# Half a token block moved in two feed-forward phases, early gate columns, and a third token-stationary input in the recurrent block

## The reference

```python
# every feed-forward layer
jnp.square(jax.nn.relu(x @ w1)) @ w2

# second block, layer 0 (recurrent)
h = _modulate(_rmsnorm(x, norm_g[layer]), shift, scale)
u, g = jnp.split(h @ w_in, 2, axis=-1)
u = causal_conv4(u) + conv_b
r  = sigmoid(_block_diag(u, w_a) + b_a)
gi = sigmoid(_block_diag(u, w_x) + b_x)
log_a = -RG_C * r * softplus(-lam)
a = exp(log_a)
b_in = sqrt(-expm1(2.0 * log_a)) * (gi * u)
hs = scan(a, b_in)                  # over tokens
y = (hs * silu(g)) @ w_out
x = x + gate[:, None, :] * y
```

## Time and profile before

| | us |
|---|---|
| median of 3 runs | 780.31 (780.28 to 780.37) |
| the profiled execution, its own time | 780.2 |
| its span in the profile | 778.4 |
| PE busy | 768.9 (99%) |
| PEld busy | 697.1 (90%) |
| DVE busy | 586.1 (75%) |
| ACT busy | 405.1 (52%) |
| POOL busy | 34.6 (4%) |

### The profile page before, as it was taken

How to read it: one execution, slowest core, us unless ns; L and a number is a source line. 1 busy time by engine, 2 the same in 40 slices (tenths; PEclk the granted TensorE clock), 3 DMA queues, 4 the chain that set the end, 5 groups by cost and what they waited for, 6 DMA issues and landing times.

```text
span 778.4 us, 12084 instructions
## 1 busy us (share of the span) xinstructions
PE 768.9 (99%) x4982; PEld 697.1 (90%) x4982; DVE 586.1 (75%) x786; ACT 405.1 (52%) x512; POOL 34.6 (4%) x66
## 2 busy tenths in 40 slices
PE   9999999999999999999999999999999999999996
PEld 9999888988998889888889988998799988999995
DVE  5886898868688697687989776676687877756754
ACT  5455235545445424875355444445649869664632
POOL 0000000000000001000000000000500051000001
PEclk9999999999999999999999999999999999999999
DMA  9877438897867731446488977876235254754102
GB/s 351 319 274 278 184 125 324 348 320 289 313 231 288 290 122 62 163 139 267 165 326 344 347 273 275 308 263 245 103 109 216 109 216 163 270 216 164 55 3 80
DMA packets 26983, 173.94 MB, mean 223 GB/s; under 512 B 3248, under 2 KB 3632, under 8 KB 7856
## 3 DMA queue, kind: packets, MB, share of 16 engines
q1 hardware_dynamic: 26640, 173.14, 60.0%
q10 hardware_dynamic: 288, 0.02, 0.0%
HBM read 172.10 MB, written 1.05 MB: 222 GB/s over the span
## 4 chain that ended last, share of the span: by engine, by line
PE 93%; DVE 3%; ACT 2%; POOL 1%; issue 0%; POOLq 0%; ACTq 0%
PE bank L578 12%; PE bank L580 12%; PE bank L579 12%; PE Y L714 10%; PE Y L716 10%; PE Y L713 10%; PE bank L1067 2%; PE bank L1068 2%; PE bank L1069 2%; PE bank L996 2%; DVE w_low L1610 1%; PE bank L816 1%; PE Y L738 1%; PE bank L610 1%; PE bank L619 1%; PE bank L611 1%
## 5 line engine op out<-in xcount | busy, mean ns | idle before, releaser
L1610 DVE TENSOR_TENSOR w_low<-raw,w_high 128x2048 fp32r<-128x2048 f32 (+3 forms) x125 | 278.5, 2238 | 65.1 <-ACT w_high L1203 62.8
L1203 ACT CAST w_high<-raw 128x2048 fp32r<-128x2048 f32 (+3 forms) x125 | 232.5, 1869 | 92.9 <-DMA raw<-weights 80.0
L578 PE MATMUL bank<-xT_h,w_high 128*128 128x256 f32 x728 | 206.5, 284 | 0.1
L579 PE MATMUL bank<-xT_l,w_high 128*128 128x256 f32 x728 | 205.8, 283 | 0.0
L580 PE MATMUL bank<-xT_h,w_low 128*128 128x256 f32 x728 | 205.8, 283 | 0.0
L578 PEld LDWEIGHTS bank<-xT_h,w_high 128*128 128x128 f32 x728 | 139.4, 192 | 1.6 <-DVE w_low L1610 0.3
L579 PEld LDWEIGHTS bank<-xT_l,w_high 128*128 128x128 f32 x728 | 139.4, 191 | 1.1
L580 PEld LDWEIGHTS bank<-xT_h,w_low 128*128 128x128 f32 x728 | 139.5, 192 | 0.0
L714 PE MATMUL Y<-w_low,hT_h 128*128 128x512 f32 x324 | 128.3, 396 | 0.0
L713 PE MATMUL Y<-w_high,hT_h 128*128 128x512 f32 x324 | 128.0, 395 | 0.0
L716 PE MATMUL Y<-w_high,hT_l 128*128 128x512 f32 x324 | 101.9, 395 | 0.0
(11 more groups left out here) (291 smaller groups left out, 1144.5 us busy)
## 6 DMA issues: line engine op xcount, KB each, us to landing
raw<-weights SPq DMA_DIRECT2D x149, 1024.0 KB, 5.0
rows<-rows_in SPq DMA_DIRECT2D x9, 512.0 KB, 7.7
raw<-weights SPq DMA_DIRECT2D x4, 576.0 KB, 3.5
z<-gates_in SPq DMA_DIRECT2D x4, 512.0 KB, 3.8
raw<-weights SPq DMA_DIRECT2D x2, 896.0 KB, 4.4
raw<-weights SPq DMA_DIRECT2D x3, 512.0 KB, 7.0
x<-x_in SPq DMA_DIRECT2D x2, 512.0 KB, 4.4
kT<-rows_in SPq DMA_DIRECT2D x2, 512.0 KB, 8.3
```

Of the source, the lines that this page charges most:

```text
L578: mm(dst, high, xh[:, kt, :], start=kt == 0, stop=False)
L579: mm(dst, high, xl[:, kt, :], start=False, stop=False)
L1203: nc.scalar.copy(w_high[:, n % RING, start:COLS[n]], raw[:, s % RAW, start:COLS[n]]).then_inc(w_high_ready, 1)
L1610: tt(w_low[:, n % RING, start:COLS[n]], slot[:, start:COLS[n]], f32(w_high[:, n % RING, start:COLS[n]]), ALU.subtract).then_inc(raw_done, 1)
```

## The change

PE, feed-forward: the first half of group 2 for block 0 is issued ahead of the transposes of block 1, and the first half of group 2 for block 1 ahead of `turn_pair(0)`. This holds for `ff0` and `ff1`.

Gate columns of layer 0: POOL makes all eight in `raw_columns`, in `ff1` behind the square of unit 0, with the bias added in the same instruction. PE turns them into rows right behind the transposes of `rs1` block 0, and ACT copies the rows ahead of the scaling of block 1. DVE's bias addition waits for the columns.

Third input: u2 is made with the tokens as the stationary side, block 0 behind the transposes of block 1, and block 1 behind u1. Then `turn_input(2)` turns it. Its weight split moves on DVE from behind the staging of block 1 to ahead of the layer norm of block 1, behind a wait for POOL's root of `rs1` block 0.

Exit: ACT and DVE split v1 and v2 one place earlier than before, and ACT also v3.

```diff
@@ unit_table
-    t.extend([("gate", 0, 0), ("gate", 0, 1), ("rg", "u", 0), ("rg", "u", 1)])
+    t.extend([("gate", 0, 0), ("gate", 0, 1), ("rg", "u", 0), ("rg", "u", 1), ("rg", "u", 2)])
@@ PE, feed_forward
                 pair_block(first[0], phase, 0, fresh)
+                up_block(first[2], PI[phase, "up", 2], 0, fresh, range(0, KT // 2))
                 transposes(fresh, x, "x_ready", [1])
-                up_block(first[2], PI[phase, "up", 2], 0, fresh)
+                up_block(first[2], PI[phase, "up", 2], 0, fresh, range(KT // 2, KT))
                 pair_block(first[1], phase, 1, fresh)
+                up_block(first[2], PI[phase, "up", 2], 1, fresh, range(0, KT // 2))
                 turn_pair(phase, 0)
                 in_order(phase, 2)
-                up_block(first[2], PI[phase, "up", 2], 1, fresh).then_inc(product, 1)
+                up_block(first[2], PI[phase, "up", 2], 1, fresh, range(KT // 2, KT)).then_inc(product, 1)
@@ PE, recurrent block
             transposes("rs1", z, blocks=[0], z_name="rs1")
+            for n in range(2):
+                gate_row(0, n)
...
             transposes("rs1", z, blocks=[1], z_name="rs1")
-            for n in range(2):
-                gate_row(0, n)
+            inputs.append(open_unit("rg", "u", 2))
+            up_block(inputs[2], PI["rg", "u", 2], 0, "rs1")
...
             up_block(inputs[1], PI["rg", "u", 1], 1, "rs1", quarter[1]).then_inc(product, 1)
+            in_order("rg", "u", 2)
+            up_block(inputs[2], PI["rg", "u", 2], 1, "rs1", quarter[0])
+            turn_input(1)
+            up_block(inputs[2], PI["rg", "u", 2], 1, "rs1", quarter[1]).then_inc(product, 1)
...
-            input_tile(2, 0, quarter[0])
-            turn_input(1)
-            input_tile(2, 0, quarter[1])
             for g in range(1, MXG + 1):
                 if g == 2:
-                    input_tile(2, 1).then_inc(u_ready, 1)
+                    turn_input(2)
@@ POOL
+            def raw_columns():
+
+                pool.wait_ge(S["token_hidden"], nth("token_hidden", "ff1", 0))
+                pool.wait_ge(raw_done, AT["mod", MOD["gate0"] // 2 + KT // 2 - 1] + 1)
+                for t in range(KT):
+                    last = nc.gpsimd.tensor_scalar(area_f[:, t * P:(t + 1) * P], ones[:, :], mcol("gate0", t),
+                                                   col("mod_b", MOD["gate0"] + t), ALU.mult, ALU.add)
+                last.then_inc(columns_ready, 2)
...
+            raw_columns()
             roots("ln3", "rs1", blocks=[0])
-            pool.wait_ge(mod_ready, 1)
-            repeated_columns(0, 0)
             first_low("rs1", 0)
             roots("ln3", blocks=[1])
             for part in (1, 2, 3):
                 first_low("rs1", part)
             roots("rs1", blocks=[1])
-            repeated_columns(0, 1)
+            pool.wait_ge(mod_ready, 1)
@@ ACT
             rms_squares("rs1", "ln3", 1)
+            act.wait_ge(S["x_ready"], nth("x_ready", "ln3", 2 * TB - 1))
+            for n in range(2):
+                await_product(act, "gate", 0, n)
+                nc.scalar.copy(rows[:, 0, n * 512:(n + 1) * 512], bank_of("gate", 0, n)[:, :]).then_inc(evacuates("gate", 0, n), 1)
             rms_scale("rs1", 1, [0])
...
-            split_ahead(("rg", "down", MXG - 1), 2)
+            split_ahead(("rg", "down", MXG - 1), 3)
             rms_squares("rs2", "rg", 0)
...
-            split_ahead(("rg", "down", MXG - 1), 3)
+            split_ahead(("rg", "down", MXG - 1), 4)
             gate_kept(0)
             rms_squares("rs2", "rg", 1)
-            split_ahead(("rg", "down", MXG - 1), 4)
@@ DVE
             def modulation_parameters():
+                dve.wait_ge(columns_ready, 2)
...
             layer_norm_apply("ln3", 0)
             modulation_parameters()
+            await_rstd("rs1", 0)
+            split_ahead(("ff1", "down", FFG - 1), 4)
             layer_norm_sums("ln3", "ff1", 1)
...
             split_transposed("rs1", 1, *modulation["rs1"])
-            split_ahead(("ff1", "down", FFG - 1), 4)
...
-            split_ahead(("rg", "down", 3), 1)
+            split_ahead(("rg", "down", 3), 2)
             gated_residual("rg", 0, 0)
             await_rstd("rs2", 0)
-            split_ahead(("rg", "down", 3), 2)
+            split_ahead(("rg", "down", 3), 3)
```

More of the change, by code:

```diff
@@ L953, in turn_input @@
                         last = nc.tensor.transpose(u_bank(g)[:, t * SEQ + b * P:t * SEQ + (b + 1) * P],
-                                                   buf_a[:, g, b * SEQ + t * P:b * SEQ + (t + 1) * P], ident)
+                                                   buf_a[:, g % 2, b * SEQ + t * P:b * SEQ + (t + 1) * P], ident)
                 last.then_inc(u_ready, 1)
@@ L1457, in gate_tanhs @@
                 last.then_inc(evacuates("rg", kind, i), 1)
-            def gate_copied(n):
-                await_product(act, "gate", 0, n)
-                nc.scalar.copy(rows[:, 0, n * 512:(n + 1) * 512], bank_of("gate", 0, n)[:, :]).then_inc(evacuates("gate", 0, n), 1)
             def input_copied(g):
                 await_product(act, "rg", "u", g)
-                nc.scalar.copy(buf_a[:, g, :], bank_of("rg", "u", g)[:, :]).then_inc(evacuates("rg", "u", g), 1)
-            act.wait_ge(S["x_ready"], nth("x_ready", "ln3", 2 * TB - 1))
-            for n in range(2):
-                gate_copied(n)
+                if g >= 2:
+                    act.wait_ge(u_ready, g - 1)
+                nc.scalar.copy(buf_a[:, g % 2, :], bank_of("rg", "u", g)[:, :]).then_inc(evacuates("rg", "u", g), 1)
             split_ahead(("rg", "g", 1), 0)
@@ L1473, in _ @@
             input_copied(1)
+            input_copied(2)
             def output_gate(i):
```

## The result

| | before | changed |
|---|---|---|
| median, us | 780.34 (780.28 to 780.44) | 783.76 (783.64 to 784.3) |
| profiled execution, us | 780.2 | 783.7 |
| its span, us | 778.4 | 781.9 |

The ratio is 1.0044, with a 95% interval of 1.0033 to 1.0056: slower by 3.4 us, where 2.8 were forecast. Timed once more beside the experiments the changed kernel came to 1.0036 (1.0024 to 1.0049).

The account below looks back on a forecast made before the run. It took PE as the bound (busy 99%, 93% of the chain of waits). `ff0` 0.48, `ff1` 0.73, recurrent block 1.5 and POOL's columns 0.1 summed to +2.8 us on 780.2: 783.0 us, range 779.0 to 784.9.

Parts of the forecast that it names:

- Feed-forward: `ff0` and `ff1`: DVE's list behind the later transposes ends later and delays `down` of block 1, +0.48 and +0.73 us.
- Columns in `ff1`: `ff1`: POOL's eight `raw_columns` instructions beside DVE's closed list cost +0.1 us, bounds 0 and 1.2 us.
- Rival 3: POOL's lock delays two modulation products in `ff1` (0.6 us each) and exit columns (some 0.3): 784.4 us, chance 0.12.
- Entry: Entry of the recurrent block, to g0: +2.12 us, including −1.31 gate rows, +1.09 early split, +2.88 u2 matmuls.
- The chain hangs on a0: Recurrent block: ACT and DVE's chain is 2.12 us later throughout; `down` (3,0) starts +0.85 us, with a wait of 1.4.
- Exit: Exit: two DVE splits ahead of the gated residual delay it 2.20 us and PE's transposes +1.9 us, 0.85 already counted.
- the root follows by 4.34 us as before: Exit: the root comes 4.34 us behind the gated residual's start, unchanged from the kernel before.
- The wait for v2's split: Exit: the earlier split on ACT removes PE's wait for v2's remainder, −0.4 us.
- The sum: Whole kernel: 0.48 + 0.73 + 1.5 + 0.1 = +2.8 us, 783.0 us; chance 0.52.
- Rival 1: Whole kernel: PE alone decides, since the lists have more air than read; −2.6 us, 777.6 us, chance 0.13.
- Rival 2: Feed-forward gains 0.6 and the block costs 1.5 (781.1 us), or feed-forward costs 1.2 and the block nothing (781.4); chance 0.23.

Follow-up runs that it names:

- Experiment 1: The kernel before with the half-block moves in feed-forward alone: 781.62 us, ratio 1.0014.
- experiment 2: The changed kernel with DVE's silu moved ahead of the remainders of block 1 in `ff1`, into DVE's wait for ACT: 782.58 us, ratio 1.0027.
- experiment 12: The changed kernel as it is, timed again: 783.32 us, ratio 1.0036.
- Experiment 11: The changed kernel with POOL's `first_low` part 1 ahead of its root of `ln3` block 1 at the entry: 783.36 us, ratio 1.0036.
- Experiments 7: The changed kernel without the third input, u2 made and split as in the kernel before: 781.45 us, ratio 1.0014.
- experiment 9: The changed kernel with group 0 in the order a0 x0 g0, on PE, ACT and DVE: 780.71 us, ratio 1.0.
- experiment 5: The changed kernel with ACT's and DVE's weight splits at the exit put back as before: 782.9 us, ratio 1.003.
- experiment 3: The changed kernel without DVE's wait for POOL's root of `rs1` block 0 ahead of u2's split: 785.24 us, ratio 1.0057.
- experiment 4: The changed kernel with u2's split behind the layer norm of block 1, and without the wait for POOL's root: 784.94 us, ratio 1.0059.
- experiment 6: The changed kernel with POOL's root of `rs2` block 0 between the two groups of four gate columns of layer 1: 786.39 us, ratio 1.0076.
- experiment 10: The changed kernel with a0 x0 g0, silu ahead of the remainders in `ff1`, exit splits and `ff0` as before: 779.66 us, ratio 0.9988.

## Why the forecast held, and where it was off

**Feed-forward: right, and shown.** The steps gave 0.48 and 0.73 us, and measured were 0.47 and 0.67. Experiment 1 has them alone (1.1 us), and experiment 2 shows that the list on DVE carries the one of `ff1`. The wait of 0.5 us for the square wasn't foreseen. It takes nothing more, because `down` of block 1 waits for the end of the same list anyway.

**Columns in `ff1`: 0.1 too much.** `raw_columns` took 7.53 us for eight instructions (9.57 in the trace of experiment 12), but DVE's modulation products beside it lasted 1.22 us as before, and the waits of experiment 1 are the same without it. POOL did the waiting. Rival 3 fails in this half.

**Entry: right in size.** The sum to g0 was +2.12 us. a0 came 2.04 later (28.57 − 26.53), with the wait of 1.04 us for `first_low` part 1 that was named at 1.1. Experiment 11 adds a point that the step had wrong in form: it put the cost at POOL's order. That order only decides where the wait is met. The layer norm behind the early split holds both.

**The chain hangs on a0: right.** The last remainder was to be 2.12 us later and was 2.06. `down` (3,0) started 0.80 us later than the entry explains, where the forecast had 0.85; PE's wait there was 1.05 us and not 1.4. Experiments 7 and 9 move a0 in the other direction, and the remainder follows.

**Exit: the mechanism was right, a term too small.** Of the transposes the forecast said +1.9 us, and they came 2.50 late. The step that failed is "the root follows by 4.34 us as before": from the start of the residual to the split that waits for the root it was 4.95 us (641.00 to 645.95). The root was not waiting for ACT's squares but for the columns ahead of it on POOL, held up by a third split of DVE. That is the half of rival 3 that came true, at 0.6 us and not 0.3. The kernels agree: the columns lasted 11.03 us with three splits beside them and 8.97 with two, and 8.89 with two in experiment 5. With two, the root had 1.50 us to spare in the kernel before and 0.35 in experiment 5. The wait for v2's split is gone, and the stretch to the end is 0.4 us shorter, as the step said.

**The sum.** The terms of one execution are 0.47 + 0.67 in the phases, 0.24 of small shifts between them up to the entry, 2.50 in the block and −0.4 behind it: 3.5 us between the spans. Against the forecast's 2.8 that is +0.6 for the root and +0.2 for those shifts, −0.1 for the columns.

**The rivals.** Rival 1 (PE alone decides, −2.6) needed more air in the chain than there was. Rival 2 needed one stage to cost nothing, and both cost what was read. In experiment 9, though, rival 1's idea shows for the block: with a0 early it takes 0.4 us less than in the kernel before (88.26 against 88.66), the wait of 1.04 us at the entry included. So with a0 first the third input no longer makes the block slower. What was dear is that its matmuls stood, with g0, ahead of the one product that the slowest chain starts from. Whether the third input gains anything isn't shown, for the kernel before was not run with a0 first.

The Trainium skill (SBUF — State Buffer, "Who interferes with whom") says that a DVE instruction with two SBUF inputs and a GpSimd one that reads SBUF lock each other out. Experiments 3, 4 and 6 agree for POOL: 2.34 us for 0.30, 4.66 for 2.50, 4.48 for 2.4. That DVE can wait in its turn showed once, in experiment 6: a split of 2.74 us at 651.55, beside the end of POOL's `first_low` and a root. In `ff1` it didn't.

**Open.** How much of experiment 10's 1.0 us belongs to the change, and how much to a0 first and the silu's new place, isn't separated. In experiments 3, 4 and 6 the clock's part is read from one execution each. The two half-block moves were not taken apart from each other, so which of them costs in `ff0` isn't shown. Nor was experiment 10 run with the early splits at the exit, which by the last column of the table would save another 0.4 us.

## What to carry to other kernels

When several engines run fixed lists, find the instruction that the slowest chain starts from, and put it ahead of everything on the busy engine that the chain doesn't need; work that fills a wait in front of it is paid twice, there and in the cover that it leaves behind. Read slack by pairs: the wait of one engine (here 2.12 us for the residual) is used up by a late chain or by an extra instruction, and the two together cost more than the sum of each. A wait that vanishes from the list is no gain until the time shows it: in experiment 11 it only changed its name. And a long wait of PE can cost more than its length: read the granted clock behind it before the loss is put down to the lists.

## What the runs showed of the hardware

A 2.3 us split on DVE that starts just ahead of POOL's root makes an instruction on 128 numbers last 2.34 us, and so costs PE a wait of 1.88. POOL's instruction ends with the split (555.89 for POOL, 555.72 for DVE), as if it had waited for all of it, and not as if it had run beside it at a lower rate. Moving either party helps only if nothing of the other's list stands in the new place, and in two of three tries (experiments 4 and 6, not 11) something did.

TensorE's granted clock makes the long waits dearer. It fell to 0.50 of full, 1.2 GHz, in three of the kernels, each time behind idle time of PE: 1.88 us in experiment 3; 0.78 and shortly after it 0.94 in experiment 4; 0.81 and then 2.10 in experiment 6. It stayed there for some 3.4 us each time. These stretches cost 1.28, 1.53 and 1.59 us more than the same matmuls took in the changed kernel, where behind waits of 1.04 us at the entry and 1.42 at the exit the clock stayed full. So of the three slowest kernels here, none was slow by its lists alone.
